# Retention in a two-layer mixer: queries and keys rotated earlier and turned by VectorE and a DRAM scratch instead of TensorE

## The reference, cut to what matters

```
q, k = columns of h @ w_in_2            # 256 x 512 each
q, k = rotary(q), rotary(k)             # x1*cos - x2*sin, x2*cos + x1*sin over the halves of each head
scores = (q k^T) * decay                # decay by distance, causal by chunks of 64
o = scores v, then a group norm over each head, times silu(gate), then a projection
```

## Time and profile before

| | |
|---|---|
| time, median of 3 runs | 1355.84 us (1354.32 to 1356.59) |
| span of the profiled execution | 1352.6 us |
| what lies around the span, by the median | 3.2 us |
| ScalarE and GpSimd busy | 55% and 4% of the span |
| loaded and stored by DMA | 226.25 MB, mean 167 GB/s |
| mean granted TensorE clock | 0.999 of full |

### The profile page before, as it was taken

One profiled execution on the slowest core, in us unless ns is written; L12 is line 12 of the kernel. 1 busy time (PEld: TensorE's weight loads), 2 busy tenths in 40 slices (PEclk: granted clock), 3 DMA queues, 4 the chain that ended last, 5 costly groups with the idle time before them and its releaser, 6 DMA issues.

```text
span 1352.6 us, 17955 instructions
## 1 busy us (share of the span) xinstructions
PE 1340.9 (99%) x7129; PEld 1146.8 (85%) x7129; DVE 935.8 (69%) x1214; ACT 746.4 (55%) x1067; POOL 58.2 (4%) x44
## 2 busy tenths in 40 slices
PE   9999999999999999999999999999999999999998
PEld 7988888978888998888878888889888887888886
DVE  6789866699867488757885555457695778655544
ACT  6864766675674565544465444456644445544432
POOL 1002000001100001000000000000100000000000
PEclk9999999999999999999999999999999999999999
DMA  8654235554345455434464655644644345466552
GB/s 292 216 168 156 94 125 187 178 165 156 109 148 181 160 198 174 156 118 150 156 218 128 186 186 171 233 156 160 207 156 136 128 157 187 137 206 187 187 176 104
DMA packets 139715, 226.25 MB, mean 167 GB/s; under 512 B 8113, under 2 KB 54897, under 8 KB 139505
## 3 DMA queue, kind: packets, MB, share of 16 engines
q1 hardware_dynamic: 137968, 222.49, 50.1%
q10 hardware_dynamic: 1664, 2.63, 0.5%
HBM read 224.05 MB, written 1.05 MB: 166 GB/s over the span
## 4 chain that ended last, share of the span: by engine, by line
PE 95%; DVE 2%; ACT 1%; issue 1%; DMA 0%; SPq 0%; ACTq 0%; DVEq 0%
PE gp L669 73%; PE gp L657 8%; PE mp L637 5%; PE mp L982 3%; PE mp L798 1%; DVE wt_rest L1579 1%; PE mp L865 1%; PE mp L840 1%; PE mp L975 1%; PE mp L819 1%; PE mp L826 1%; ACT first_hi L1177 1%; DMA wt<-in_w_mem_kv 0%; DVE arena L1573 0%; DVE arena L1576 0%
## 5 line engine op out<-in xcount | busy, mean ns | idle before, releaser
L1579 DVE TENSOR_TENSOR wt_rest<-wt,wt_hi 128x1024 fp32r<-128x1024 f32 x148 | 174.4, 1221 | 83.0 <-ACT wt_hi L1177 81.3
L1177 ACT ACTIVATE wt_hi<-wt 128x1024 fp32r<-128x1024 f32 x148 | 148.1, 1053 | 97.1 <-DMA wt<-in_ffn_down 48.5
L1177 ACT ACTIVATE mix_hi<-wt 128x1024 fp32r<-128x1024 f32 x128 | 132.1, 1060 | 103.7 <-PE gp L669 74.7
L1579 DVE TENSOR_TENSOR wt_rest<-wt,mix_hi 128x1024 fp32r<-128x1024 f32 x128 | 151.1, 1221 | 35.1 <-ACT mix_hi L1177 34.1
L1579 DVE TENSOR_TENSOR wt_rest<-wt,first_hi 128x1024 fp32r<-128x1024 f32 x104 | 124.0, 1221 | 25.8 <-ACT first_hi L1177 24.9
L669 PE MATMUL gp<-mix_hi,mix_hT_hi 128*128 128x512 f32 x352 | 139.9, 397 | 0.0
L669 PE MATMUL gp<-wt_rest,mix_hT_hi 128*128 128x512 f32 x352 | 137.1, 390 | 0.0
L669 PE MATMUL gp<-mix_hi,mix_hT_rest 128*128 128x512 f32 x352 | 133.4, 390 | 0.0
L669 PE MATMUL gp<-wt_hi,hT_hi 128*128 128x512 f32 x320 | 126.7, 396 | 0.0
L1177 ACT ACTIVATE first_hi<-wt 128x1024 fp32r<-128x1024 f32 x104 | 105.8, 1059 | 36.9 <-PE gp L669 26.1
L669 PE MATMUL gp<-wt_hi,hT_rest 128*128 128x512 f32 x320 | 124.9, 390 | 0.0
(11 more groups left out here) (347 smaller groups left out, 2933.6 us busy)
## 6 DMA issues: line engine op xcount, KB each, us to landing
wt<-in_w_in SPq DMA_DIRECT2D x96, 1024.0 KB, 5.1
wt<-in_w_out SPq DMA_DIRECT2D x20, 1024.0 KB, 5.1
wt<-in_ffn_gate SPq DMA_DIRECT2D x40, 512.0 KB, 4.0
wt<-in_ffn_up SPq DMA_DIRECT2D x40, 512.0 KB, 5.0
wt<-in_ffn_down SPq DMA_DIRECT2D x20, 1024.0 KB, 5.1
wt<-in_w_mem_kv SPq DMA_DIRECT2D x7, 1024.0 KB, 5.2
arena<-in_w_in SPq DMA_DIRECT2D x4, 1024.0 KB, 8.1
wt<-in_w_branch_pool SPq DMA_DIRECT2D x4, 1024.0 KB, 5.0
```

The costliest lines, as they stand in the source:

```text
L1177: nc.scalar.activation(rounded_part(u)[:, k:k + nk, :], raw_of(u)[:, k:k + nk, :], ACT.Copy)\
L1579: return nc.vector.tensor_tensor(o, i0, i1, ALU.subtract)
```

## The change

The rotation of retention's queries and keys moves on VectorE from level 0 up to the place behind the rests of unit 13, ahead of the delta rule's norms. Behind it VectorE has two new instructions, one for the queries and one for the keys. Each turns all 32 by 32 blocks of a 128x1024 region in place of one another, block by block, and writes to G0 and G1. The blocks are then in themselves transposed but still stand at their old places in the 4 x 4 grid of each 128 x 128 tile. A trip through DRAM puts them right: behind the load of unit 18 SP writes the two regions to a scratch (2 DMAs, 1,024 rows of 512 bytes each), and behind the load of unit 19 it waits for the writes and reads the scratch back over RQ and RK (8 DMAs of 32 partitions, each partition 32 runs of 128 bytes). TensorE's 16 transposes and ScalarE's four copies per layer go, and the scores wait for the reads (`ret_back`).

```diff
--- before.py
+++ after.py
@@ -115,7 +115,7 @@
     + ["hg0_0", "hg0_1", "hg8", "qmT0", "qmT1"] + [f"ms{h}" for h in range(4)] + [f"mpt{h}" for h in range(4)] + ["qaT0", "qaT1", "kaT0", "kaT1"] \
     + ["om0", "om1", "hgo0", "hgo1"] + [f"sc{h}" for h in range(4)] + ["yT4", "yT5"] + [f"sc{h}" for h in range(4, 8)] + ["yT2", "yT3"] \
     + [f"pt{h}" for h in range(8)] + ["oa0", "oa1", "yT0", "yT1"]
-BETWEEN = {1: ["rqT0", "rqT1", "rkT0", "rkT1"], 2: ["rs0", "rs1", "rs2"], 3: ["ro0", "ro1", "pm0", "pm1"], 4: ["py0", "py1"]}
+BETWEEN = {2: ["rs0", "rs1", "rs2"], 3: ["ro0", "ro1", "pm0", "pm1"], 4: ["py0", "py1"]}
 ORDER_2 = [f"xT{i}" for i in range(4)] + ["ba", "bat", "cg", "gb0", "gb1"] \
     + [f"bT{j}{t}" for j in range(3) for t in range(2)] \
     + ["kT0", "kT1", "mm0", "mm1", "at0", "at1", "mi"] \
@@ -342,6 +342,8 @@
         xs2 = region(b_e, TT, D)
         sq2 = region(b_e, 2048)
         sg = region(b_tmp, 2, 2, S)
+        ret_turned = [region(R2[g], 2 * NH, P) for g in ("G0", "G1")]
+        ret_far = nc.dram_tensor("ret_far", (2 * DEPTH, 2 * NH, P, P), F, kind="Internal").ap()
 
 
         def part(name, at, *shape):
@@ -409,6 +411,7 @@
         pow_asked, pow_given = sem("pow_asked"), sem("pow_given")
         v_chain, a_chain = sem("v_chain"), sem("a_chain")
         out_done = sem("out_done")
+        ret_written, ret_back = sem("ret_written"), sem("ret_back")
         w_rounded, w_split = sem("w_rounded"), sem("w_split")
         named = {}
         pow_widths = []
@@ -547,6 +550,7 @@
         def load_place(u):
             return ("staged", staged_half(u)) if u in STAGED_UNITS else ("ring", slot_of(u))
 
+        ret_after = {MIX_UNITS[l][18 + i]: (l, i) for l in range(DEPTH) for i in range(2)}
         place_total = collections.Counter()
         unit_value = []
         for u in range(len(UNITS)):
@@ -609,6 +613,19 @@
                     sp.dma_start(const[:, c0:c1], w["shape_constants"][:, c0:c1]).then_inc(loaded["const2"], 16)
                 for dst, src in unit_loads(u):
                     sp.dma_start(dst, src).then_inc(load_signal(u), 16)
+                if u in ret_after:
+                    l, i = ret_after[u]
+                    if i == 0:
+                        for n, turned in enumerate(ret_turned):
+                            sp.wait_ge(sig("ret_rotated"), 2 * l + n + 1)
+                            sp.dma_start(ret_far[2 * l + n].rearrange("m q c -> q m c"), turned).then_inc(ret_written, 16)
+                    else:
+                        sp.wait_ge(ret_written, 16 * 2 * (l + 1))
+                        for n, g in enumerate(("RQ", "RK")):
+                            far = ret_far[2 * l + n].rearrange("m (p i) (j r) -> j i (m p) r", p=4, j=4)
+                            near = region(R2[g], 1024).rearrange("q (b r) -> q b r", r=32)
+                            for q in range(4):
+                                sp.dma_start(near[32 * q:32 * q + 32], far[q]).then_inc(ret_back, 16)
             for t in range(TT):
                 sp.wait_ge(sig("x_tile"), 2 * (3 * DEPTH) - TT + t + 1)
                 sp.dma_start(out[0, t * P:(t + 1) * P, :], x[:, t, :]).then_inc(out_done, 16)
@@ -988,15 +1005,10 @@
                     if fill:
                         g, c = fill.pop(0)
                         split_units(s(g), c)
-                def retention_transposes():
-                    for n, g in (("rqT", "RQ"), ("rkT", "RK")):
-                        for t in range(TT):
-                            transposes(s(f"{n}{t}"), [reg("B", g)[:, t, P * q:P * q + P] for q in range(4)], (sig("ret_rotated"), l + 1))
-
                 def retention_scores():
                     for i, (jt, it) in enumerate(((0, 0), (0, 1), (1, 1))):
                         quad(s(f"rs{i}"), lambda h: reg("B", "RK")[:, jt, P * h:P * h + P], lambda h: reg("B", "RQ")[:, it, P * h:P * h + P],
-                             *[read_out(s(f"{n}{t}")) for n in ("rqT", "rkT") for t in range(TT)])
+                             (ret_back, 16 * 8 * (l + 1)))
 
                 def retention_values():
                     for t in range(TT):
@@ -1030,7 +1042,7 @@
                 def values_and_means():
                     retention_values()
                     pool_means()
-                between = {1: retention_transposes, 2: retention_scores, 3: values_and_means, 4: pool_mix}
+                between = {2: retention_scores, 3: values_and_means, 4: pool_mix}
                 def branch(name):
                     split_units(s(name), 1)
                 transposes(s("mi"), [ml[:, h, :] for h in range(NH)], (sig("level_ready"), len(LEVELS) * l + 1))
@@ -1484,10 +1496,6 @@
                         round_weights(parts_until(MIX_UNITS[l][0] + 19) - 1)
                     if g is not None:
                         move(s(g), ACT.Sigmoid if g[0] == "G" else ACT.Silu)
-                    if n == 1:
-                        for m, q in (("rqT", "RQ"), ("rkT", "RK")):
-                            for t in range(TT):
-                                evacuate(f"{m}{t}", reg("B", q)[:, t, :], bank(s(f"{m}{t}")))
                     if n == 3:
                         for t in range(TT):
                             evacuate(f"ro{t}", reg("B", "RQ")[:, t, :], bank(s(f"ro{t}")))
@@ -2122,6 +2130,22 @@
                 rests_until(11)
                 convolve(2)
                 rests_until(13)
+                dve.wait_ge(loaded["const2"], 16)
+                dve.wait_ge(*group_in("RQ"))
+                dve.wait_ge(*group_in("RK"))
+                rr = region(R2["RQ"], 4, NH, P)
+                x1, x2 = rr[:, :, :, 0:64], rr[:, :, :, 64:P]
+                cosv, sinv = (C(n_).rearrange("p (a j) -> p a j", a=4)[:, :, None, :].to_broadcast([P, 4, NH, 64]) for n_ in ("cos", "sin"))
+                ta = region(R2["G0"], 4, NH, 64)
+                tb = region(R2["G1"], 4, NH, 64)
+                v(mul(ta, x1, sinv))
+                v(mul(tb, x2, sinv))
+                v(mul(x1, x1, cosv))
+                v(sub(x1, x1, tb))
+                v(mul(x2, x2, cosv))
+                v(add(x2, x2, ta))
+                for n, turned in enumerate(ret_turned):
+                    nc.vector.transpose(turned, region(R2[("RQ", "RK")[n]], 2 * NH, P)).then_inc(sig("ret_rotated"), 1)
                 kv, vv = heads(reg("B", "K")), heads(reg("B", "V"))
                 q_scale, q_square = small[:, 136:144], small[:, 144:152]
                 sq16 = sq2.rearrange("p (n d) -> p n d", n=16)
@@ -2193,23 +2217,6 @@
                                 mul(invT[:, t], both_inv, upper_lower[:, t][:, None, :].to_broadcast([P, NH, P])).then_inc(sig("inverse"), 1)
                     if n < 6:
                         rests_until(18 + 2 * n)
-                    if n == 0:
-
-                        dve.wait_ge(loaded["const2"], 16)
-                        dve.wait_ge(*group_in("RQ"))
-                        dve.wait_ge(*group_in("RK"))
-                        rr = region(R2["RQ"], 4, NH, P)
-                        x1, x2 = rr[:, :, :, 0:64], rr[:, :, :, 64:P]
-                        cosv, sinv = (C(n_).rearrange("p (a j) -> p a j", a=4)[:, :, None, :].to_broadcast([P, 4, NH, 64]) for n_ in ("cos", "sin"))
-                        ta = region(R2["G0"], 4, NH, 64)
-                        tb = region(R2["G1"], 4, NH, 64)
-                        v(mul(ta, x1, sinv))
-                        v(mul(tb, x2, sinv))
-                        v(mul(x1, x1, cosv))
-                        v(sub(x1, x1, tb))
-                        rests_until(19)
-                        v(mul(x2, x2, cosv))
-                        add(x2, x2, ta).then_inc(sig("ret_rotated"), 1)
                     if n == 2:
                         for i, dst in enumerate((rst[:, 0], rst[:, 1], rst_late[:, :, :])):
                             dve.wait_ge(*computed(s(f"rs{i}")))
```

## The result

| | before | after |
|---|---|---|
| median | 1355.08 us (4 runs, 1353.99 to 1356.59) | 1366.82 us (4 runs, 1365.57 to 1368.11) |
| ratio | | 1.0090, 95% interval 1.0078 to 1.0102 |
| span of the profiled execution | 1352.6 us | 1366.3 us |
| mean granted clock | 0.999 | 0.995 |

The changed kernel is slower by 11.7 us; 12.7 were forecast, 1368.5 us against 1366.8. Thirty-nine later runs of the kernel before, timed for the experiments, have medians of 1354.2 to 1354.5, so the 11.7 may be up to 0.9 too small. The changed kernel's profiled execution is one of the two longer runs (1368.11), so its span shows 13.7 us. Each run since lists its own span, and what lies around it is 1.8 us, not 3.2: the profiled execution of the kernel before was a short one, of about 1354.4 us, and the 3.2 compared it with the median.

A forecast was written before the change was run, and what follows sets the result against it. TensorE, busy 99% of 1352.6 us, was taken as the bound; per layer 6.1 stall + 2.0 clock - 1.77 transposes = +6.35, two layers +12.7 on median 1355.84: 1368.5 us, range 1362 to 1378.

The forecast's parts named there:

- Transposes: TensorE's sixteen transposes per layer, ahead of quad Y2, are removed: 1.77 us won per layer, 3.54 us for two.
- Insertion: On VectorE behind unit 13's rests: six rotation passes 7.5 us, two turns 2.3 us, 9.8 us in all.
- Stall: TensorE ahead of unit 14 (RG's first half): 6.9 us pushed back less 0.76 slack, 6.1 us standing still per layer.
- Clock: Behind the stall TensorE runs some microseconds at half rate: between nothing and 3.3 us lost, 2.0 taken per layer.
- The wait at unit 17: TensorE waits another 0.8 us for unit 17's rests, unless it has lost as much in the meantime.
- The rival in which the clock holds: No half-rate stretch behind the stall; unit 17 adds 0.8: 5.1 per layer, +10.2, 1366.1 us; chance 0.27.
- DRAM trip: Scratch writes and reads on SP's queue, 18 ns per packet taken, 6 us of cover before unit 20: cost nothing.
- the rival of late reads: From 29 ns a packet reads outlast their cover; at 78.6 ns unit 20 comes 25 us late, twice: 1419; chance 0.13.
- the estimate by that figure: Scratch reads priced by the skill's 19 times and a 1 MB load's 5.1 us: 97 us, kernel some 1530.
- Sum: Per layer 6.1 + 2.0 - 1.77 = +6.35 us; two layers +12.7: span 1365.3, median 1368.5 us.
- The 3.2 us around the span: Difference between the profiled span of 1352.6 us and the timed runs' median 1355.84, taken as lying around the span.
- The other side: Insertion absorbed by VectorE's gap and the slack before unit 14, 3.7 us; with no stall 1352.3; chance 0.05.

The follow-up runs named there:

- spread_2: Changed kernel with rotation passes spread over VectorE's gaps, unit 12's rests first, turns in level 0, DRAM trip behind units 21 and 22: 1351.15 us, ratio 0.9975.
- its twin with transposes: Kernel before with only the rotation spread over the same gaps, unit 12's rests first; no turns, no trip, 16 transposes kept: 1353.94 us, ratio 0.9995.

## Why the prediction was right

- **Transposes, 1.77 us per layer.** Right: 3.65 us for both layers in the run without transposes, and the difference of `spread_2` and its twin with transposes is 2.8 us, somewhat less.
- **Insertion, 9.8 us.** Right: 7.55 + 2.30. The turn of 128x1024 was the unknown duration; the step of 1.15 us that was taken is what the trace shows.
- **Stall, 6.1 us.** Right: 6.06 in each layer, and 3.7 in the run with the rotation alone ahead, 5.9 ahead of the keys in the run with the insertion behind unit 14.
- **Clock, 2.0 us per layer.** Right in kind: 2.66 and 2.05 in the profiled execution. That the size fits is in part luck. It was chosen between nothing and 3.3, and behind the same wait of 6.1 us the stretch at half rate differs: 13 and 10 products in the changed kernel's two layers, 14 and 10 without the trip, 12 and 9 with runs of 64 bytes, 8 and 14 with runs of 32. By the steps above, 8 to 14 products cost 1.7 to 2.9 us. The wait at unit 17 was swallowed, as said, and appears once the clock is held. The rival in which the clock holds failed here, but with a wait of 2.8 us the clock did hold once in four.
- **DRAM trip, nothing.** Right. The packet price was put at 18 ns and is 13.0 by the same measure; the rival of late reads needed 29 and has its edge at about 35, by the estimate above. The Trainium skill ("VectorE: DVE Perf Modes", The three transpose paths) says of a plain DMA which transposes by strides that it is 19 times slower than the hardware's transposing DMA when the innermost stride on the destination is large. The prediction left that condition out, and it isn't met here: the run of 32 floats that VectorE's turn leaves intact is contiguous on both sides, so the packets stay at 128 bytes, and SP's issues of the reads took 5.93 us, where the estimate by that figure had 97. No run here transposes element by element, so the rule itself is not tested. Shorter runs did bring a cost, from some point between 64 and 32 bytes.
- **Sum.** 6.1 + 2.0 - 1.77 = 6.35 per layer. From RG's first product to G3's the first layer shows 558.64 - 515.88 = 42.76 us before and, between 516.57 and 566.32, 49.75 after: 7.0, and 6.3 in the second layer. By medians the change costs 5.9 per layer, which is what the shortest stretches at half rate would give.
- **Level.** Two things are off in 1368.5 beside the 12.7. The 3.2 us around the span should be 1.8, which changes nothing in a sum that starts from the median; and that median, of three runs, was about 1.5 us above the medians of the 39 later ones. The range was stated a little wider (1362 to 1378) than its own terms give (1362.7 to 1376.4); the measured time lies inside both.
- **The other side** (absorbed) failed in the changed kernel, since eight passes of 1.2 us don't fit 3.7 us. But it named the right quantity: with the six passes of the rotation laid out over VectorE's gaps, 8.3 us of them, and the two turns in level 0, where the rotation had stood, the absorption is real and the kernel gains.

What isn't settled: the four timed runs of the changed kernel fall in two pairs, near 1368 and near 1365.6. The stretch at half rate does differ from profile to profile, by up to 1.2 us per layer, which is enough for the 2.4 us between the pairs; but only one of the four runs was profiled, so that this is their cause is not shown. Nor is it shown what decides how long the stretch is, or whether a wait of 2.8 us costs the clock.

## What to carry to other kernels

When TensorE is fed by another engine's in-order queue, price an insertion there by the first thing behind it that TensorE waits for, less the gap ahead of it and the slack of that thing; freeing the engine elsewhere does not count. Work of many small passes can be laid into several gaps, but look up between which two instructions, not which two calls, each gap lies. And add to a stall of 3.7 us or more the half-rate stretch behind it: here a quarter to a half of the stall again.

## What the runs showed of the hardware

- Waits of 3.7 us and more were all followed by products at 1.2 GHz, six to fourteen of 128x512 in steps of 0.427 us where such products came first. Of four waits of 2.8 us three were and one was not; waits of 1.1 and 0.7 us were not. The same wait of 6.1 us was followed by 8 to 14 such products, depending on the execution.
- VectorE turns 128x1024 floats in blocks of 32 by 32 in 1.15 us, the price of a pass with two operands over as many elements; the plain copy of the earlier trace rows took 0.69.
- Loads from DRAM in short scattered runs passed one packet per engine every 11.6, 12.0 and 11.5 ns at 128, 64 and 32 bytes, all three by the length of SP's issues: the number of packets set the time, and halving the run doubled it.
